# Cached keys turned inside the recurrences' turns; long and short query tiles alternate in the attention

## The reference

```python
def _band_attn_prompt(q, k, v, table):
    '''Each 64-frame chunk attends to its own chunk and the previous 8 chunks (gathered band).'''
...
def _band_attn_sample(q, k, v, k_cache, v_cache, table):
    kk = jnp.concatenate([k_cache.astype(k.dtype), k], axis=1)
    vv = jnp.concatenate([v_cache.astype(v.dtype), v], axis=1)
...
    s = jnp.einsum('bqhd,bkhd->bhqk', q, kk).astype(jnp.float32) * (hd ** -0.5) + bias
    p = jax.nn.softmax(jnp.where(valid, s, -jnp.inf), axis=-1).astype(vv.dtype)
    return jnp.einsum('bhqk,bkhd->bqhd', p, vv).reshape(B, L, H * hd)
```

## Time and profile before

| | us |
|---|---|
| median of 3 runs | 3515.36 (3512.35 to 3522.54) |
| profiled execution, its own time | 3515.92 |
| span of the profiled execution | 3514.3 |
| PE busy in the span | 3317.9 (94%) |
| DVE busy | 1328.4 (38%) |
| POOL busy | 1037.0 (30%) |
| ACT busy | 725.1 (21%) |
| mean granted clock of PE | 0.973 |

### The profile page before, as it was taken

How to read it: one execution, slowest core, us unless ns; L and a number is a source line. 1 busy time by engine, 2 the same in 40 slices (tenths; PEclk the granted TensorE clock), 3 DMA queues, 4 the chain that set the end, 5 groups by cost and what they waited for, 6 DMA issues and landing times. The chain is left out here.

```text
span 3514.3 us, 63125 instructions
## 1 busy us (share of the span) xinstructions
PE 3317.9 (94%) x26930; PEld 3071.5 (87%) x26930; DVE 1328.4 (38%) x1724; ACT 725.1 (21%) x1270; POOL 1037.0 (30%) x675
## 2 busy tenths in 40 slices
PE   7999977888799999999999999899999999999997
PEld 7978856777599999999999998566699999999997
DVE  5630045555543333333334110355524333333333
ACT  3212122332321000000002001466513000000004
POOL 3452053442204233222234331011033222322223
PEclk8989978999899999999999999999999999999999
DMA  5222122110612111111111233565411111111101
GB/s 198 76 82 80 50 69 62 45 45 15 194 34 69 42 36 40 43 54 42 36 36 50 89 107 115 162 177 149 122 48 61 42 42 36 36 42 55 43 27 54
DMA packets 271472, 246.44 MB, mean 70 GB/s; under 512 B 23689, under 2 KB 236258, under 8 KB 271289
## 3 DMA queue, kind: packets, MB, share of 16 engines
q1 hardware_dynamic: 264152, 217.43, 19.6%
q0 software_dynamic: 7136, 26.35, 2.5%
HBM read 191.70 MB, written 54.13 MB: 70 GB/s over the span
## 5 line engine op out<-in xcount | busy, mean ns | idle before, releaser
L390 PE MATMUL PS<-hT_high,w_split_tiles 128*128 128x384 f32 x5856 | 1188.8, 335 | 4.3 <-POOL w_split_tiles L573 2.0
L390 PEld LDWEIGHTS PS<-hT_high,w_split_tiles 128*128 128x128 f32 x5856 | 1029.5, 188 | 6.2 <-POOL w_split_tiles L573 2.9
L390 PE MATMUL PS<-hT_low,w_split_tiles 128*128 128x384 f32 x2928 | 665.6, 334 | 0.0
L390 PE MATMUL PS<-ffn_act_split,w_down_split 128*128 128x384 f32 x3024 | 530.3, 335 | 5.7 <-issue 4.9
L390 PEld LDWEIGHTS PS<-ffn_act_split,w_down_split 128*128 128x128 f32 x3024 | 526.5, 188 | 6.6 <-issue 5.2
L390 PEld LDWEIGHTS PS<-hT_low,w_split_tiles 128*128 128x128 f32 x2928 | 522.7, 188 | 0.0
L820 DVE TENSOR_TENSOR xT<-xT,PS 128x1152 f32<-128x1152 f32 x168 | 227.5, 1354 | 290.3 <-PE PS L390 290.3
L570 POOL CAST w_split_tiles<-w_raw_tiles 128x1024 fp32r<-128x1024 f32 x44 | 46.9, 1067 | 432.1 <-PE PS L390 320.3
L570 POOL CAST w_split_tiles<-attention_oT 128x1024 fp32r<-128x1024 f32 x42 | 43.7, 1042 | 331.1 <-PE PS L390 312.9
L760 ACT CAST ffn_act_split<-ffn_room 128x1152 fp32r<-128x1152 f32 x22 | 25.6, 1164 | 483.2 <-PE PS L390 347.7
L760 ACT CAST ffn_act_split<-attention_oT 128x1152 fp32r<-128x1152 f32 x22 | 25.6, 1164 | 478.5 <-PE PS L390 347.7
(11 more groups left out here) (445 smaller groups left out, 4808.4 us busy)
## 6 DMA issues: line engine op xcount, KB each, us to landing
w_raw_tiles<-in_ffn_w_gu_dram SPq DMA_DIRECT2D x44, 512.0 KB, 3.9
attention_oT<-in_ffn_w_gu_dram SPq DMA_DIRECT2D x44, 512.0 KB, 3.8
cache_k<-in_cache_c_k_dram SPq DMA_DIRECT2D x64, 256.0 KB, 4.9
cache_v<-in_cache_c_v_dram SPq DMA_DIRECT2D x64, 256.0 KB, 4.9
ffn_room<-in_ffn_w_down_dram SPq DMA_DIRECT2D x11, 1024.0 KB, 6.0
attention_oT<-in_ffn_w_down_dram SPq DMA_DIRECT2D x11, 1024.0 KB, 5.9
rest_dram<-w_raw_tiles SPq DMA_DIRECT2D x36, 256.0 KB, 2.1
w_raw_tiles<-in_c_w_qkv_dram POOLq DMA_DIRECT2D x18, 512.0 KB, 4.5
```

What stands on the lines that cost most here:

```text
L390: m = nc.tensor.matmul(PS[:, banks + j, 0:GN], wl if p == 2 else wh, sl if p == 1 else sh, start=(n == 0 and p == 0), stop=(n == last and ...
```

## The change

The cached keys are turned in `recurrences`, in 32 units. A unit is one pair of heads and two streams: SP loads it (two transfers of 256 KB), PE makes 8 transposes into banks 1 and 2, ACT copies both banks back over the loaded keys in one instruction, and SP stores them (512 KB) to a new DRAM tensor kT. Turns 0 to 7 have three units each, turn 8 four, and the last turn (`s` = 8 alone) four. Loads for a turn are issued at the end of the turn before, behind its stores. The buffers are a new tile and tiles that are free at that time. `keep_warm` is taken out. PE waits for the copy before each next unit and before `a_pairs`; POOL, ACT and DVE wait once, at k = 1, for stores out of buffers that they are about to write.

In `attention` the key turns, their copies, `cache_k` and its loads are gone. `cache_kT` has two buffers, each filled by one transfer of 2 MB. The query tiles are visited in the order 4, 0, 5, 1, 6, 2, 7, 3, samples; `step(g)` gives the pair, the tile t and the position u.

```diff
+        def place_of(x):
+
+            return (x % 3, x // 3) if x < EARLY else (x % 4, (x - EARLY) // 4 + (EARLY // 3 if x % 4 < 3 else 0))
...
+            def load_keys(x):
+                s, use = place_of(x)
+                if use:
+                    sp.wait_ge(keys_out[s], 16 * use)
...
+                for y in range(2):
+                    sp.dma_start(to[:, y], cache_k[2 * b + y].rearrange("(r p) c -> p r c", p=P)[:, :, i * P:(i + 1) * P]
+                                 ).then_inc(keys_in[s], 16)
+
+            def store_keys(x):
+                s, use = place_of(x)
+                i, b = divmod(x, BS // 2)
+                sp.wait_ge(keys_kept, x + 1)
+                sp.dma_start(e.scr["kT"][i][:, 2 * b:2 * b + 2], keys(x).rearrange("p (b r) -> p b r", b=2)
+                             ).then_inc(keys_out[s], 16)
...
                 if n is not None and n + 1 < NT:
                     load(n + 1)
+                for x in units(at_):
+                    store_keys(x)
+                if at_ < NT:
+                    for x in units(at_ + 1):
+                        load_keys(x)
...
             def a_pairs(k):
                 tready.wait(pe, k)
                 dec_exp.wait(pe, k)
+                if k:
+                    pe.wait_ge(keys_kept, units(k - 1)[-1] + 1)
                 gram(k, kbt[:], a_mm)
...
-            def keep_warm(n, count):
-
-
-                dec_exp.wait(pe, n)
-                for _ in range(count):
-                    mm(PS[:, 1, :], spr[:, 0:P], spr[:, 0:512], start=True, stop=True)
+            def turn_keys(c, y):
+                x = units(c)[y]
+                s, use = place_of(x)
+                if c < NT - 1:
+                    dec_exp.wait(pe, c + 1)
+                else:
+                    pt_ready.wait(pe, NT - 1)
+                pe.wait_ge(keys_in[s], 32 * (use + 1))
+                if x:
+                    pe.wait_ge(keys_kept, x)
+                k = keys(x)
+                for b in range(2):
+                    for j in range(NK):
+                        z = pe.transpose(PS[:, 1 + b, j * P:(j + 1) * P], k[:, (b * NK + j) * P:(b * NK + j + 1) * P], ident)
+                z.then_inc(keys_turned, 1)
...
                 if i is not None:
+                    turn_keys(i, 0)
+                if s == NT - 1:
+                    turn_keys(NT, 0)
+                if i is not None:
                     z_blocks(i, 2)
                 if s is not None:
                     outputs(s)
+                if s == NT - 1:
+                    turn_keys(NT, 1)
...
+                if s == NT - 1:
+                    turn_keys(NT, 2)
+                    turn_keys(NT, 3)
...
-                if i is not None and n is not None:
-                    keep_warm(n, 3)
+                if i is not None:
+                    turn_keys(i, 1)
                 if n is not None:
                     turn_qk(n, 2)
-                if i is not None and n is not None:
-                    keep_warm(n, 4)
+                if i is not None:
+                    turn_keys(i, 2)
                 if i is not None:
                     z_half(i)
                     pairs(i, 1)
                     du_half(i)
+                if i == NT - 1:
+                    turn_keys(i, 3)
...
+            def keep_keys(c, y):
+                x = units(c)[y]
+                act.wait_ge(keys_turned, x + 1)
+                copy(keys(x), PS[:, 1:3, :].rearrange("p b n -> p (b n)")).then_inc(keys_kept, 1)
...
                     keep_qk(n, 1)
+                if i is not None:
+                    keep_keys(i, 1)
+                if n is not None:
                     keep_qk(n, 2)
                 if i is not None:
+                    keep_keys(i, 2)
                     keep_z_half(i)
...
+    TILES = [4, 0, 5, 1, 6, 2, 7, 3, SAMPLE]
...
-                for b in range(BS):
-                    n = i * BS + b
-                    if n >= 4:
-                        sp.wait_ge(cache_turned, n - 3)
-                    sp.dma_start(kc[:, b % 4], ck[b].rearrange("(r p) c -> p r c", p=P)[:, :, i * P:(i + 1) * P]
-                                 ).then_inc(kc_in[b % 4], 16)
+                sp.dma_start(kct[:, s], e.scr["kT"][i]).then_inc(kct_in[s], 16)
...
-                if g < NG and t < 4:
-                    cache_turn(i, 2 * t)
-                    cache_turn(i, 2 * t + 1)
-                if t == 1 and i:
+                if u == 1 and i:
                     out_turn(i - 1)
...
-                if t < 4:
-                    cache_keep(i, 2 * t)
-                    cache_keep(i, 2 * t + 1)
...
-                if t == 5 and i + 1 < NPAIR:
+                if u == 5 and i + 1 < NPAIR:
                     streams(i + 1)
```

More of the change, by code:

```diff
@@ L1693, in gla_rows, with units, keys @@
             return slice(GK * (h % 4), GK * (h % 4) + GK), h // 4
+        def units(c):
+            if c < 0:
+                return range(0)
+            return range(3 * c, 3 * c + 3) if c < NT - 1 else range(EARLY + 4 * (c - NT + 1), EARLY + 4 * (c - NT + 2))
+        def place_of(x):
+            return (x % 3, x // 3) if x < EARLY else (x % 4, (x - EARLY) // 4 + (EARLY // 3 if x % 4 < 3 else 0))
+        def keys(x):
+            s = place_of(x)[0]
+            if s == 0:
+                return first_keys[:].rearrange("p b r -> p (b r)")
+            if x < 6:
+                return decayed_states[:].rearrange("p a c -> p (a c)") if s == 1 else ob[:, 1]
+            if s == 3:
+                return Ss[:, 0:2].rearrange("p m b v -> p (m b v)")
+            return (wts if s == 1 else qts)[:].rearrange("p x m t -> p (x m t)")
         def each(turn):
@@ L1721, in sample_states_out @@
                                  .rearrange("b p v -> p b v"), GSs[:, m]).then_inc(states_out, 16)
+            def load_keys(x):
+                s, use = place_of(x)
+                if use:
+                    sp.wait_ge(keys_out[s], 16 * use)
+                if x in (7, 8):
+                    (v_mm if s == 1 else qs_mm).wait(sp, 0)
+                if s == 3 and use == 0:
+                    sp.wait_ge(states_out, 16 * 6)
+                i, b = divmod(x, BS // 2)
+                to = keys(x).rearrange("p (b r c) -> p b r c", b=2, r=NK)
+                for y in range(2):
[3 more added lines that the diff above has]
+                s, use = place_of(x)
+                i, b = divmod(x, BS // 2)
+                sp.wait_ge(keys_kept, x + 1)
+                sp.dma_start(e.scr["kT"][i][:, 2 * b:2 * b + 2], keys(x).rearrange("p (b r) -> p b r", b=2)
+                             ).then_inc(keys_out[s], 16)
             def turn(i, n, s):
+                at_ = NT if s == NT - 1 else i if i is not None else -1
                 if s is not None:
@@ L1750, in _ @@
             sp.wait_ge(o_out[1], 16 * 4)
+            for x in units(NT):
+                s, use = place_of(x)
+                sp.wait_ge(keys_out[s], 16 * (use + 1))
         @block.gpsimd
@@ L3116, in attention @@
     for g in range(NG):
-        i, t = divmod(g, STEPS)
-        if t < 4:
-            for b in (2 * t, 2 * t + 1):
-                chunk_of["cache", i, b] = len(engine_of)
-                engine_of.append("act")
-        if t == 1 and i:
+        i, t, u = step(g)
+        if u == 1 and i:
             chunk_of["out", i - 1, 0] = len(engine_of)
@@ L3153, in attention @@
         qk_in, near_in, v_in, rows_in = two("pair_qk_in"), two("pair_near_in"), two("pair_v_in"), two("pair_near_rows_in")
-        kc_in = [e.sem(ctx, f"cache_k_in{n}") for n in range(4)]
+        kct_in = two("cache_kT_in")
         vc_in, zeroed, prepared, samples_prepared, streams_ready = e.sem(
@@ L3327, in _ @@
         def _(act):
-            def cache_keep(i, b):
-                chunk = chunk_of["cache", i, b]
-                act.wait_ge(chunk_turned, chunk + 1)
-                if i:
-                    for grp in range(2):
-                        act.wait_ge(score_mm[grp], i * STEPS)
-                nc.scalar.copy(kct[:, b], PS[:, bank(chunk), :]).then_inc(kept["act"], 1)
             def keep(g, x):
@@ L3409, in reduce @@
             def reduce(g, hp):
-                i, t = divmod(g, STEPS)
+                i, t, u = step(g)
                 w = widths(min(t, 4))
-                if t in (0, SAMPLE) and hp == 0:
-                    dve.wait_ge(prepared if t == 0 else samples_prepared, i + 1)
+                if (u == 0 or t == SAMPLE) and hp == 0:
+                    dve.wait_ge(prepared if u == 0 else samples_prepared, i + 1)
                 dve.wait_ge(score_mm[hp], g + 1)
```

88 lines of the change are left out of this document (49 added, 39 removed).

## The result

The changed kernel took 3458.86 us (median of 4 runs, 3456.52 to 3471.93), the kernel before 3515.42 us (4 runs, 3512.35 to 3522.54). The ratio is 0.9844, with a 95% interval of 0.9815 to 0.9873: 56.6 us less by the medians. The forecast was 48 us less, 3467 us, with a range of 3453 to 3492.

What follows compares the result with a forecast made beforehand. PE was taken to bound the attention and, with holes, lead the recurrences. Terms: -59.5 + 1.0 + 1.0 (attention) + 1.0 (steady turns) + 1.5 (early turns) + 7.0 (end) = -48.0, giving 3467 us, range 3453 to 3492.

Steps and rivals of the forecast that it cites:

- The attention: Pairs of heads: removing key turns saves 59.5 us; the first long tile costs 1.0 us, stalls 1.0 us.
- The 0.15 us of stall a pair: Attention: PE waits left in the new tile order, taken from a likely 0 to 0.3 us; 1.0 us in all.
- Rival B: Attention: DVE and ACT latency makes short steps wait, losing 32 of the 59.5 us, kernel 3499 us; chance 13%.
- my margin of 0.1 us: Attention, new order: second head's transposes at 4.2 us at the earliest, against the long tile's second exponential ending at 4.11.
- Rival C: Attention: DMA is late for the pair, a stall of 2 us a pair, kernel 3483 us; chance 5%.
- Steady turns: Recurrences: three key units fit holes of PE, costing 0 to 0.3 us a turn, 1 us over eight turns.
- Early turns: Recurrences' two early turns: units cost double at the lower clock, samples' turn lacks a state product; 1.5 us more.
- The end: Recurrences' last turns, without cover for the units: next stage starts 7 us later, bounds 3 and 13.
- up to 8 us for a gain of clock: Part of the range 3453 to 3492: the recurrences' last turns might gain clock, up to 8 us.
- the signs that I named: Pairs 31.5 to 32 us, turns 44.4 to 44.8 at clock 1.00, z_half unmoved, next stage 8 to 12 us later.
- rival A: Recurrence turns: without fillers the clock falls, kernel about 3628 us if wholly low; chance 5%, milder form (3480 to 3510) 7%.
- my 20 us for a whole one: Recurrences: a turn wholly at the lower clock level takes some 20 us more, 160 us for eight.

Runs made afterwards that it cites:

- e1: Attention of after with recurrences of before, the keys loaded as the cache lies and turned nowhere, against the kernel before: 3462.55 us, ratio 0.9834.
- e4: The kernel before without both keep_warm calls (seven idle matmuls a turn), nothing in their place: 3544.93 us, ratio 1.0060.
- e6: The kernel before with four more idle matmuls ahead of z_blocks(i, 2) in each recurrence turn but the last: 3509.59 us, ratio 0.9970.
- e7: The changed kernel without the last turn's four key units, their loads and stores: 3450.67 us, ratio 0.9806 against the kernel before.
- e5: The kernel before, with SP waiting on the key transposes' semaphore itself in place of PE: 3498.60 us, ratio 0.9935.
- e2: Recurrences of after (keys turned and stored there) with the attention of before, against the kernel before: 3520.22 us, ratio 0.9999.

## Why the prediction was right, and which term was off

**The attention** (-59.5, +1.0 and +1.0, so -57.5): right, and for the reason given. The measured stretch is 58.7 us shorter, e1 58.5 by the times. PE's pieces add up: 31.54 worked out, 31.56 measured. The 0.15 us of stall a pair were 0.06 (31.62 - 31.56), and they came from the transfer of k_pair, which I had at 20.2 us against a need at 20.3, and not from the latency through DVE and ACT. Rival B didn't come about: PE is busy for all of the 31.56 us of a pair, and even the natural order costs only 0.34 us a pair more, so my margin of 0.1 us was far too narrow a reading. Rival C's late transfer occurred in one pair of six, at 0.4 us in place of 2 us in each.

**Steady turns** (+1.0 for eight): five turns cost 222.9 - 222.1 = 0.8 us more, 1.2 for eight at that rate. The holes were cover, each as named: four of five turns are as long as before.

**Early turns** (+1.5): this is the mis-sized term, and it has the wrong sign. The step that failed: "The two early turns run partly at the lower clock level, where a unit costs twice as much". The units cost nothing there; they kept the clock up, and the first turns became 181.1 - 174.8 = 6.3 us shorter. I had written that transposes let the clock rise and did not carry it into the sum: I used the clock as a price of the new work and not as something that the new work sets. The granted clock over them went from 0.81 to 0.85 in the two executions compared. At 0.81 some 69 of 180 us are low, at 0.85 some 52 of 174; with what e4 pays, 3.4 us for some 10 us low, the 16 us less come to some 5 us, an estimate, of the 6. e6 shows the same effect, 4.2 us, by work without any use.

**The end** (+7.0, bounds 3 and 13): 62.7 - 56.8 = 5.9 us, e7 puts 5.2 of them on the last turn, where I had 5. But the same end takes 54.0 to 59.8 us in three executions without units, so the term is known to 3 us and no better. That scatter goes with the clock; here the end in e1, before and e5:

```profile
848.12:902.07 53.95, 35.60 (x776) 32.14 (x774) 23.48 (x42) 7.19 (x16) 4.14 (x5) 0.83 0.08 25
849.18:905.87 56.69, 38.70 (x775) 34.85 (x774) 23.47 (x42) 7.20 (x16) 4.14 (x5) 0.75 0.07 24
844.71:904.50 59.79, 41.80 (x776) 37.45 (x774) 23.48 (x42) 7.19 (x16) 4.15 (x5) 0.70 0.07 23
```

The four executions with the changed kernel's end are at 0.82 to 0.85. Set against e1, at 0.83, the units of the end cost 8.7 us, an estimate from one execution; so it seems that here too they raised the clock, and paid for a part of themselves.

Together the four come to -58.7 + 0.8 - 6.3 + 5.9 = -58.3 us, measured -56.6 by the medians; forecast -48.0. Nearly all of the difference is the early turns. The range's lower part had up to 8 us for a gain of clock, but in the last turns and not in the first; that 3458.86 lies in it is to that extent luck.

Of the signs that I named, the pair's distance, z_half and the steady turns but one (45.41 us) came as written. The next stage's start did not (2.8 us earlier, not 8 to 12 later), nor did the clock of 1.00 in every turn: the first distance from decay to decay had 0.96.

**The clock, rival A.** It didn't come about, and the reason I gave against it, that PE gets at least as much work in the same places as it loses, is what e4 and e2 bear out. Its price for e4 was near: a turn with 10 of its 48 us low costs 4.2 us at my 20 us for a whole one, and 3.4 were measured. Its chance of 12% rested on the right question, which e4 would have answered ahead of the change; the fillers that decide it are 2 us of a turn, in two gaps.

## What to carry to other kernels

Work that has to be done somewhere is best put into the gaps of another stage where the engine waits anyway; here the 24 units of eight turns cost about 1 us before what the clock gave back, and the four that stood in a turn without cover 5 us, until they too were spread. Before work or fillers are taken out of a gap, look at the granted clock behind it, and count the clock on both sides of the sum: what fills a gap can pay for itself. Look also for an engine that waits for its own last instruction: here it cost 0.51 us each time, and moving the wait to SP, which needs it, gave half of what moving all the work gave.

## What the runs showed of the hardware

- Transposes of 128 x 128 in 32 bits held TensorE's clock nearly as the 512-column matmuls did: five turns of 44.67 us on average at 0.99 with units in the gaps (e2), of 44.43 at 1.00 with the matmuls (before), of 47.87 at 0.89 with nothing there (e4).
- Two gaps of 1.20 and 1.56 us close together were followed by some 10 us at 1.2 GHz (0.50) in the turns of e4; with the matmuls there, the same place reads 1.00 (before).
- The recurrences' end takes 54.0, 56.7 and 59.8 us in three executions of the same code, at a mean granted clock of 0.83, 0.75 and 0.70. Why the same code is granted a different clock was not found.
